# Three norms of a fused three-block kernel, taken through the halves of the tokens

## The reference, cut to what matters

```python
def rmsnorm(x, g):
    y = xf * lax.rsqrt(jnp.mean(xf * xf, axis=-1, keepdims=True) + EPS)
...
# end of the first block, start of the second
h_res = h_res + merged @ w_out[l]
return rmsnorm(h_res[:, N_META:], final_g)
n = rms_norm(x, mix_norm_g[l]); proj = n @ w_in[l]
...
# second block: its MLP, and its end
x = x + mixed @ w_out[l]
hdn = jnp.square(jax.nn.relu(rms_norm(x, mlp_norm_g[l]) @ w_up[l]))
x = x + hdn @ w_down[l]
return rms_norm(x, final_norm_g)
```

## Time and profile before

| | us |
|---|---|
| median of 3 runs (lowest, highest) | 3868.13 (3867.46, 3868.78) |
| the profiled execution | 3866.86 |
| its span, first to last instruction | 3865.5 |
| PE busy in it | 3718.8 |
| DVE, ACT, POOL busy | 1653.6, 1149.6, 1063.7 |
| mean granted TensorE clock | 0.982 of 2.4 GHz |

### The profile page before, as it was taken

How to read it: one execution, slowest core, us unless ns; L and a number is a source line. 1 busy time by engine, 2 the same in 40 slices (tenths; PEclk the granted TensorE clock), 3 DMA queues, 4 the chain that set the end, 5 groups by cost and what they waited for, 6 DMA issues and landing times.

```text
span 3865.5 us, 41782 instructions
## 1 busy us (share of the span) xinstructions
PE 3718.8 (96%) x17644; PEld 3038.5 (79%) x17644; DVE 1653.6 (43%) x2017; ACT 1149.6 (30%) x1442; POOL 1063.7 (28%) x708
## 2 busy tenths in 40 slices
PE   6999999999999989999999999998999999999998
PEld 6889887888878866777778888887777778888886
DVE  5564525999643244224232222224557652222226
ACT  5554522222231333444121111212332341111123
POOL 3333321222233531102322222222112442222223
PEclk9999999999999989999999999999999999999999
DMA  2000011111232221011211111112111221111112
GB/s 101 28 28 28 28 66 60 55 55 55 71 141 88 98 83 35 33 33 33 87 33 49 49 44 49 44 50 85 33 34 35 102 71 45 49 49 44 49 44 77
DMA packets 60666, 216.68 MB, mean 56 GB/s; under 512 B 6720, under 2 KB 6848, under 8 KB 60352
## 3 DMA queue, kind: packets, MB, share of 16 engines
q1 hardware_dynamic: 60480, 214.01, 16.7%
HBM read 188.82 MB, written 25.17 MB: 55 GB/s over the span
## 4 chain that ended last, share of the span: by engine, by line
PE 87%; DVE 7%; ACT 2%; issue 2%; POOL 1%; DMA 1%; SPq 0%; DVEq 0%; ACTq 0%
PE psum L464 76%; PE psum L576 2%; PE psum L798 2%; PE psum L813 2%; PE psum L828 1%; PE psum L528 1%; PE psum L513 1%; DVE Ab L1950 1%; DVE qb L1996 0%; POOL hl L2841 0%; PE psum L661 0%; DVE k L2538 0%; PE psum L698 0%; DVE hl L1853 0%; PE psum L600 0%
## 5 line engine op out<-in xcount | busy, mean ns | idle before, releaser
L2824 POOL TENSOR_TENSOR wl<-raw,wh 128x512 fp32r<-128x512 f32 x588 | 810.2, 1399 | 2365.7 <-ACT wh L1101 2365.7
L464 PE MATMUL psum<-hh,wh 128*128 128x512 f32 (+2 forms) x3760 | 1163.7, 392 | 63.0 <-POOL wl L2824 13.6
L464 PE MATMUL psum<-hh,wl 128*128 128x512 f32 (+2 forms) x3760 | 1124.4, 382 | 0.0
L464 PE MATMUL psum<-hl,wh 128*128 128x512 f32 (+2 forms) x3760 | 1120.7, 381 | 0.0
L464 PEld LDWEIGHTS psum<-hh,wh 128*128 128x128 f32 x3760 | 676.1, 191 | 212.3 <-issue 38.8
L464 PEld LDWEIGHTS psum<-hh,wl 128*128 128x128 f32 x3760 | 699.6, 190 | 136.6
L464 PEld LDWEIGHTS psum<-hl,wh 128*128 128x128 f32 x3760 | 698.8, 190 | 134.1
L1101 ACT ACTIVATE wh<-raw 128x1024 fp32r<-128x1024 f32 x294 | 309.7, 1053 | 772.4 <-PE psum L464 765.8
L464 PE MATMUL psum<-hdh,wh 128*128 128x512 f32 x1024 | 328.3, 398 | 4.4 <-DVE B L2725 4.4
L2378 DVE TENSOR_TENSOR B<-B,psum 128x1024 f32<-128x1024 f32 x114 | 139.2, 1221 | 444.8 <-PE psum L464 444.8
L464 PE MATMUL psum<-hdh,wl 128*128 128x512 f32 x1024 | 326.0, 395 | 0.0
(11 more groups left out here) (405 smaller groups left out, 3016.2 us busy)
## 6 DMA issues: line engine op xcount, KB each, us to landing
raw<-in_wts SPq DMA_DIRECT2D x294, 512.0 KB, 3.5
keep_x<-B SPq DMA_DIRECT2D x16, 512.0 KB, 3.8
X<-in_xin SPq DMA_DIRECT2D x8, 520.0 KB, 5.2
keep_sz<-tmp SPq DMA_DIRECT2D x8, 512.0 KB, 2.9
av<-keep_gr SPq DMA_DIRECT2D x8, 512.0 KB, 3.2
tmp<-keep_sz SPq DMA_DIRECT2D x8, 512.0 KB, 3.6
av<-keep_gc SPq DMA_DIRECT2D x8, 512.0 KB, 3.8
av<-in_xin SPq DMA_DIRECT2D x8, 512.0 KB, 3.6
```

The lines of the kernel that those rows point to most:

```text
L464: ins = pe.matmul(out, w, x[:, k, c0:c0 + width], start=first and n == 0, stop=final and n == 2)
L2824: gp.tensor_tensor(wl[:, s, a], raw[:, s, a], fp(wh[:, s, a]), SUB).then_inc(*c.lo.tick(i, p))
```

## The change

The three norms (`o1`/`o2` between `OUT1` and `SGU`, `n5` between `OUT2` and `MLP2`, `n6` between `MLP2` and `GATES3`) are taken through the two halves of the tokens.

- Slabs 4 to 7 of `OUT1` and of `OUT2`, the four down slabs of the last group of `MLP2`, the four slabs of `SGU`, the first four up slabs of `MLP2`, and the first four of block 3 (gates, `pre` 0 and 1, `v` of head 0) are run for each half of the tokens in turn. Their 24 weights are fetched and split twice: 318 slabs instead of 294.
- PE sums a half of the tokens and spreads its row as side jobs (`rest_out`, `rest_square`) some steps into the next half's slabs.
- DVE adds all squares; POOL adds none any more. DVE reads the spread rows in PSUM (no copies by ACT), by halves of a tile. `hh` and `hl` are made by halves; POOL keeps tiles 3, 5 and 7.
- The fourth `aux` bank is there from the end of `OUT1` on. `xn` and `xb` are new SBUF buffers. The side job `spatial` starts after the first half of `SGU` with other pauses; the gates' transposes become a side job beside the slab of head 0's output gate.
- SP's order of fetches, loads and stores is rewritten; the first norm's results are stored by halves for tiles 6 and 7.

The core of the diff, blank lines left out:

```diff
-SGU, QKV, SHORT, OUT2, MLP2 = 96, 100, 112, 118, 126
-GATES3, HEADS3, POOL3, OUT3, MLP3 = 190, 191, 207, 211, 223
-NSLAB = 294
-WEIGHTS = (list(range(219)) + list(range(215, 223)) + list(range(219, 283)) + list(range(280, 283)))
-TWICE = {MLP2: 0, MLP3: 4}
+SGU, QKV, SHORT, OUT2, MLP2 = 100, 108, 120, 126, 138
+GATES3, POOL3, OUT3, MLP3 = 210, 231, 235, 247
+NSLAB = 318
...
+WEIGHTS = [*range(92), *twice(92, 96), *twice(96, 100), *range(100, 122), *twice(122, 126), *twice(126, 130),
+           *range(130, 186), *twice(186, 190), *twice(190, 194), *range(194, 215), *twice(215, 219), *twice(219, 223),
+           *range(223, 280), *twice(280, 283)]
+HALVED = {MLP2: 0, MLP3: 1}
...
-            gemm(OUT1 + m, c.ev_v("out", m), last=(m == 7))
-        pe.wait_ge(*c.acc_v("o1", 7))
-        token_sums("o1", Cb[:, 0, :])
-        pe.wait_ge(*c.acc_v("o2", 7))
-        token_sums("o2", Cb[:, 1, :])
-        pe.wait_ge(*c.inv("o2"))
-        spread("o2", 1)
-        spread("o1", 0)
-        duo(SGU, "nx2", [c.ev("sv", 0), c.ev("sv", 1)])
...
+        def rest_out(hf):
+            yield from pause(6)
+            x = grab(aux, ("tok", "o", hf), c.inv("o2", hf, "mean"))
+            for n, st in enumerate(("o1", "o2")):
+                pe.wait_ge(*c.acc_v(st, 7, hf))
+                for z in range(4):
+                    a = hf * 512 + z * 128
+                    ins = pe.matmul(x[:, 4 * n + z:4 * n + z + 1], Cb[:, n, a:a + 128], ones[:, 0:1], start=True, stop=True)
+            ins.then_inc(*c.tok.tick("o", hf))
+            yield from pause(6)
+            for st, slot, last in (("o2", 1, c.nrm("nx2", 7, hf)), ("o1", 0, c.nrm("x1", KEEP_X[-1], hf))):
+                x = grab(aux, ("row", st, hf), last)
+                pe.wait_ge(*c.inv(st, hf))
+                half_spread(st, hf, slot, x)
+        for m in (2, 3):
+            gemm(OUT1 + m, c.ev_v("out", m))
+        for hf in range(2):
+            for m in range(4, 8):
+                gemm_half(OUT1 + 4 * hf + m, hf, c.ev_v("out", m, hf))
+            side.drain()
+            side.add(rest_out(hf))
...
-        side.add(pause(8))
-        job = side.add(spatial())
-        for m in range(2):
-            gemm(SGU + 2 + m, c.ev("su", m))
+        job = None
+        for hf in range(2):
+            for n in range(4):
+                until = c.ev("sv", n, hf) if n < 2 else c.ev("su", n - 2, hf)
+                gemm_half(SGU + 4 * hf + n, hf, until, "nx2" if n == 0 else None)
+            if hf == 0:
+                side.drain()
+                job = side.add(spatial())
...
-        pe.wait_ge(*c.acc_v("n5", 7))
-        token_sums("n5", acc5)
-        pe.wait_ge(*c.inv("n5"))
-        spread("n5", 0)
...
+        def rest_square(st, hf):
+            yield from pause(4)
+            x = grab(aux, ("tok", st, hf), c.root(st, hf))
+            pe.wait_ge(*c.acc_v(st, 7, hf))
+            for n in range(4):
+                a = hf * 512 + n * 128
+                ins = pe.matmul(x[:, n:n + 1], acc5[:, a:a + 128], ones[:, 0:1], start=True, stop=True)
+            ins.then_inc(*c.tok.tick(st, hf))
+            yield from pause(2)
+            x = grab(aux, ("row", st, hf), c.nrm("ff2" if st == "n5" else "fin2", 7, hf))
+            pe.wait_ge(*c.inv(st, hf))
+            half_spread(st, hf, 0, x)
...
+        for hf in range(2):
+            for m in range(4, 8):
+                gemm_half(OUT2 + 4 * hf + m, hf, c.ev_v("x2", m, hf))
+            side.drain()
+            side.add(rest_square("n5", hf))
+        def first_ups(base, ver):
+            for hf in range(2):
+                for u in range(4):
+                    gemm_half(base + 4 * hf + u, hf, c.ev("up", base, u, hf), ver if u == 0 else None)
+                side.drain()
...
+        def last_downs(base, hf, xh, xl):
+            for j in range(HALVED[base], 4):
+                i, prs = down_at(base, 7, j, hf), [None, None]
+                for e, k in DOWN_FIRST if j == 0 and hf == 0 else DOWN_REST:
+                    if k == 0:
+                        prs[e] = grab(pairs, (i, e), c.ev_v("dn", base, 7, 2 * j + e, hf))
+                    if j == 0 and e == 0:
+                        pe.wait_ge(*c.ml_dve("lo", base, 28 + k))
+                    ins = three(prs[e], None, i, k, 4 * e + k, k == 0, k == 3, xh, xl, 0, (hf,))
+                    if k == 3:
+                        ins.then_inc(*c.gemm.tick(i, e))
+                    side.turn()
+            side.drain()
+        first_ups(MLP2, "ff2")
         mlp(MLP2, hdh, hdl)
-        pe.wait_ge(*c.acc_v("n6", 7))
-        token_sums("n6", acc5)
-        pe.wait_ge(*c.inv("n6"))
-        spread("n6", 0)
-        duo(GATES3, "nx3", [c.ev("gates"), c.ev("pre", 0, 0)])
+        for hf in range(2):
+            last_downs(MLP2, hf, hdh, hdl)
+            side.add(rest_square("n6", hf))
...
+        for hf in range(2):
+            for n in range(4):
+                until = (c.ev("gates", hf), c.ev("pre", 0, 0, hf), c.ev("pre", 0, 1, hf), c.ev("v3", 0, hf))[n]
+                gemm_half(GATES3 + 4 * hf + n, hf, until, "nx3" if n == 0 else None)
+            side.drain()
...
-                gemm(i, c.ev("pre", h, 0))
-            gemm(i + 1, c.ev("pre", h, 1))
-            gemm(i + 2, c.ev("v3", h))
-            if h == 0:
-                gate_columns()
-            gemm(i + 3, c.ev("o3", h))
+                gemm(heads_at(h, 0), c.ev("pre", h, 0))
+                gemm(heads_at(h, 1), c.ev("pre", h, 1))
+                gemm(heads_at(h, 2), c.ev("v3", h))
+            else:
+                job = side.add(gate_columns())
+            gemm(heads_at(h, 3), c.ev("o3", h))
...
+        for m, tiles in ((5, (0, 1)), (6, (2, 3, 4)), (7, (5, 6))):
+            split(OUT1 + m + 5)
+            squares_out(m - 1, 1)
+            for k in tiles:
+                out_high(k, 0)
+        squares_out(7, 1)
+        split(SGU + 1)
+        out_high(7, 0)
+        roots_out(1)
...
+        out(0)
+        out(1)
+        out(2)
+        add_out(1)
+        out(3)
+        add_out(2)
+        out(4, 0)
+        add_out(3)
+        for m in (5, 6, 7):
+            out(m, 0)
+            add_out(m - 1, 0)
+        add_out(7, 0)
+        out_stats(0)
         ve.wait_ge(*c.small("gmix"))
-        ve.wait_ge(*c.row("o2", 1))
-        for k in range(KT + 1):
-            if k < KT:
-                q = Cb[:, 4 + (14 + k) % 4, :]
-                if k >= 4:
-                    ve.wait_ge(*low_done("nx2", k - 4))
-                ve.scalar_tensor_tensor(q, X[:, k, :], gmix[:, k:k + 1], Cb[:, 3, :], MUL,
-                                        MUL).then_inc(*c.nrm.tick("nx2", k))
+        for m, tiles in ((4, (0, 1, 2)), (5, (3, 4, 5)), (6, (6, 7)), (7, ())):
+            out(m, 1)
+            if m > 4:
+                add_out(m - 1, 1)
+            for k in tiles:
+                out_norm(k, 0)
+                if k:
+                    out_low(k - 1, 0)
+        out_low(7, 0)
+        out_kept(6, 0)
+        out_kept(7, 0)
+        add_out(7, 1)
+        for k in KEEP_X[2:]:
+            out_kept(k, 0)
+        out_stats(1)
+        for k in range(KT):
+            out_norm(k, 1)
             if k:
-                low("nx2", k - 1, Cb[:, 4 + (13 + k) % 4, :])
-        ve.wait_ge(*c.row("o1", 1))
-        for k in range(KT):
-            ve.scalar_tensor_tensor(X[:, k, :], X[:, k, :], V("final_g", k), Cb[:, 2, :], MUL,
-                                    MUL).then_inc(*c.nrm.tick("x1", k))
+                out_low(k - 1, 1)
+        out_low(7, 1)
+        for k in KEEP_X:
+            out_kept(k, 1)
...
+        for m in (5, 6, 7):
+            mixed_in(m, 0)
+            add_mean_square("n5", m - 1, 0)
+        add_mean_square("n5", 7, 0)
+        mean_stats("n5", 0)
+        for m, tiles in ((4, (0, 1, 2)), (5, (3, 4, 5)), (6, (6, 7)), (7, ())):
+            mixed_in(m, 1)
+            if m > 4:
+                add_mean_square("n5", m - 1, 1)
+            for k in tiles:
+                mlp_norm(k, 0)
+                if k:
+                    mlp_low(k - 1, 0)
+        add_mean_square("n5", 7, 1)
+        mlp_low(7, 0)
+        mean_stats("n5", 1)
+        for k in range(KT):
+            mlp_norm(k, 1)
             if k:
-                low("ff2", k - 1, t5[:, 3 + (6 + k) % 3, :])
+                mlp_low(k - 1, 1)
+        mlp_low(7, 1)
...
+        for hf, tiles in ((0, {}), (1, {2: (0, 1), 3: (2,), 4: (3, 4), 5: (5,), 6: (6, 7)})):
+            for m in range(8):
+                last_group(m, hf)
+                if m > 1:
+                    add_mean_square("n6", m - 1, hf)
+                if (m, hf) == (0, 1):
+                    mean_stats("n6", 0)
+                for k in tiles.get(m, ()):
+                    block_norm(k, 0)
+                    if k:
+                        block_low(k - 1, 0)
+            add_mean_square("n6", 7, hf)
+        block_low(7, 0)
+        mean_stats("n6", 1)
+        for k in range(KT):
+            block_norm(k, 1)
```

(40 more changed lines are left out.)

725 lines of the change are left out of this document (410 added, 315 removed).

## The result

| | before | changed |
|---|---|---|
| median of runs | 3867.8 us (3866.29 to 3868.78, 4 runs) | 3816.49 us (3815.74 to 3818.15, 4 runs) |
| profiled execution: its time, its span | 3866.9 us, 3865.5 us | 3818.15 us, 3816.8 us |
| mean granted clock of TensorE | 0.982 | 0.986 |

The changed kernel takes 0.9868 of the time before (95% interval 0.9851 to 0.9885), 51.3 us less by the medians. The prediction was 3814 us, 3800 to 3830, with 0.95 for faster.

What follows compares the result with a forecast made beforehand. PE, busy in 96% of the span, bounds the kernel and loses 85.4 us around three norms; 31.1 us comes back, so a 54.3 us gain from 3866.9 gives 3812.6, median 3814 us; range 3800 to 3830, forecast 3803 to 3824 at 0.60.

Steps and rivals of the forecast that it cites:

- Small matmuls: Sums and spreads of halves at the three norms, in line on PE with nothing to hide them: 15.3 us put back.
- First norm: Between OUT1 and SGU: PE waits 2.4 us, mainly for DVE's last additions, and loses 1.8 us to the clock.
- Spatial gate: During SGU: its chain of about 17.5 us gets 15.3 us of PE steps, so 1.5 us of waiting is added.
- Second norm: Between OUT2 and MLP2: DVE has one addition for a tile and nearly keeps up; 0.5 us put back.
- Third norm: Between MLP2 and GATES3: DVE falls behind, 4.3 us of waits, 1.8 us of clock, 0.5 us for the last hdl.
- Gates' chain: Behind the third norm: the chain on 4 partitions stays, its 3.63 us wait and slow clock shrink; 3.0 us left.
- Slabs by halves at no cost: Half passes keep 0.232 us a matmul, and the weights of 24 more slabs are covered: 0 us put back.
- Rival 3: Weights become the bound in the 48 half passes, each waiting 2 us: slower, 3894 us; chance 0.03.
- Rival 2: DVE bounds each half pass, additions near 1.78 us, lag at all three norms: 3825 to 3832 us; chance 0.22.
- Rival 1: DVE keeps up, no new wait, only the 15.3 us comes back: 3798 us; chance 0.13.

Runs made afterwards that it cites:

- all_orders: The changed kernel with seven moves in the engines' orders (gates, spatial gate, VectorE at the first and third norm) and the same work: 3802.94 us.

## Why the prediction was right, and where it was not

The time lies 2.5 us above the forecast of 3814, inside its own range of 3803 to 3824, and the mechanism was the one named: stops between stages became short insertions. Point by point, by its terms (what comes back of 85.4 us):

- *Small matmuls, 15.3 us: right, a little high.* At the second norm, whose window holds nothing else, both halves lose 3.2 us (3.8 said). The loss of 10.0 us at the first norm less the wait of 1.56 leaves 8.4 us (7.7 said), with the spatial gate's first transposes in it.
- *First norm, 2.4 us of waiting and 1.8 of clock: too much by 2.6 us, and its reason only half right.* The wait is 1.56 us, for `wl`, with the clock at 1.00. The forecast wait for the sums was real: it shows as 0.86 + 0.56 us once the weights come first. What the step missed is that one late VectorE gives PE two waits in a row, of which the earlier gives it time for the later. Its price for an addition, 1.10 us, was right where it was used: by form the eight of the second half, from 1357 to 1383, take (5.4 + 2.9 + 0.7) / 8 = 1.13 us; the six of the first half are shorter, the mean of all 14 from 1340 to 1400 is 0.92. `hl` was priced like the norm, 0.75 us, though it reads two operands in SBUF as the additions do: its five in that window take 0.87 us in the mean.
- *Spatial gate, +1.5 us: the wait was right, the term too small.* The 17.5 us taken for its chain stand on no row. 2.71 us against 1.15 before is 1.56 more, but taking the wait away gave 4.3 us, 3.1 more than the old wait: the slow matmuls behind it were left out, +1.6.
- *Second norm, 0.5 us: right.* PE waits for nothing, with additions at 0.73 us.
- *Third norm, 4.3 us, 1.8 of clock and 0.5 for the first down slab: 6.6 said, 5.4 found.* The loss of 8.1 us less four short groups (3.2 us, as at the second norm) leaves 4.9 us, of which 2.69 are the wait for `wl`, and slow matmuls are most of the rest; `hdl` was waited for 0.52 us. Cause as at the first norm: pair and addition are behind the weights' wait, and show as 1.0 and 1.5 us without it.
- *Gates' chain, 3.0 us left: the step that failed.* It left 6.06 us of stall, 1.46 us for `wl` ahead of it and about 2 us of slow matmuls, 9.5 us. The prediction took the chain's length as it was and only asked what lies beside it. But handing over in halves put the second half of `pre` behind ScalarE's logarithms and with it the taps ahead of the gates' work on VectorE: the chain grew from 22.2 to 30.6 us. The work beside it on PE, from the gates' row to their columns, is as long as before (2687.60 - 2662.90 = 24.7 us, 2731.63 - 2706.54 = 25.1), so the 2.9 us that PE had in hand turned into a stall. The step also misread its own row: the 3.63 us before were for `wl`, not for this chain. The changed orders of the two engines tell this; the prediction did not follow them at this place.
- *Slabs by halves at no cost: right.* The window of the second norm, half passes throughout, has room for its four short groups beside 0.232 us a matmul and for nothing else; the waits for `wl` stand at single places with GpSimd's low parts ahead of them, not in each pass. Rival 3 did not come.

In this order the misses are -0.5 (the loss of 8.4 + 3.2 + 3.2 us against 15.3), -2.6, +1.6, -0.5, -1.2 and +6.5 us, +3.3 in all, and the gain came out 3.0 us under the forecast of 54.3. That the time came so near is in part luck: the term that failed was too low by 6.5 us, and two others, at the first and the third norm, were too high by 3.8 us together. Rival 2, VectorE as the bound, is what additions_twice shows one step further: with a second instruction behind each addition the time is 3840. Rival 1, with no new wait, stands near all_orders, 3803 against 3798, though that kernel also loses waits which the kernel before had.

## What to carry to other kernels

When a stage hands over in halves, read anew every queue behind it: an instruction that needs the whole of a tensor moves behind whatever its producer does between the halves, and drags along all that stands after it. A stall of several us can be held by several in-order queues at once; its name changes with each repair and most of its time comes back only with the last (2.1 us after two repairs, 5.6 after three), so judge an edit by a stretch between two fixed points and not by the wait that went away. And before a wait is costed, ask which later wait it hides. Read too what a wait before the change is for: one that stands beside a chain need not be that chain's.

## What the runs showed of the hardware

- VectorE's 128x512 instructions with two operands in SBUF take 0.68 to 0.74 us without GpSimd beside them and up to 1.78 us with it, within microseconds of each other; the same norm with one operand in PSUM stays at 0.74 us in all 16 rows.
- The slow clock behind a wait doesn't scale with the wait. After 6.06 us at the gates TensorE ran slowly for under 10 us in one kernel, after 6.01 us in another for some 40 us (0.82 to 0.95 granted), 4 us dearer; two waits of 0.86 and 0.56 us were followed by it, one of 1.56 us was not. The clearest case is the wait of 2.69 us at the end of the attention, with the same work ahead and behind: it cost 0, 1.6 or 4.3 us of slow matmuls. What decides between these was not tried. It makes a few us of any such change hard to predict, and it took back most of what all_orders lacks of the sum of its parts.
